# A fused decoder layer with expert retrieval: the first head searched as soon as it is scored, and a quarter of the rows scaled by ScalarE and added up by GpSimd

## What is computed

```python
def hybrid_mixer(x, ...):
    h = x @ w_in                                   # q, k, v, pooling input, gates
    o = diff_attention(q[0], q[1], k[0], k[1], v, lam, slopes)   # 8 heads, causal, ALiBi
    attn_branch = (rms_norm(o) * (1 - lam_init)) @ w_attn_proj
    pool_branch = (pooled @ pool_w * pool_scale) @ w_pool_proj
    return (g_attn * attn_branch + g_pool * pool_branch) @ w_out

def peer_ffn(y, w_q, sub_keys, u, v):              # per chunk of 128 tokens
    s = einsum(y @ w_q, sub_keys)                  # 8 retrieval heads, 2 x 128 keys
    s1, i1 = top_k(s[:, :, 0], 16); s2, i2 = top_k(s[:, :, 1], 16)
    sc, ci = top_k(s1[..., :, None] + s2[..., None, :], 16)
    idx = row * 128 + col; gate = softmax(sc)      # 128 experts per token
    act = gelu(einsum('ched,cd->che', u[idx], y))
    return einsum('che,ched->cd', gate * act, v[idx])

h = layer_norm(ALPHA * h + hybrid_mixer(h)); h = layer_norm(ALPHA * h + peer_ffn(h))
```

## Time and profile before

| | |
|---|---|
| median of 3 runs | 3364.09 us (3360.29 to 3366.54) |
| profiled execution | 3356.24 us, span 3354.3 us |
| granted clock of PE, mean | 0.957 |
| PE busy | 2827.1 us, 84% of the span |
| DVE busy | 2472.8 us, 74% |
| ACT busy | 1159.0 us, 35% |
| POOL busy | 1349.3 us, 40% |
| gathers' queue | 1073.81 MB, 79.1% of the time of 16 engines |
| other loads and stores | 169.11 MB, 13.5% |
| HBM read and written | 371 GB/s over the span |

### The profile page before, as it was taken

One profiled execution on the slowest core, in us unless ns is written; L12 is line 12 of the kernel. 1 busy time (PEld: TensorE's weight loads), 2 busy tenths in 40 slices (PEclk: granted clock), 3 DMA queues, 4 the chain that ended last, 5 costly groups with the idle time before them and its releaser, 6 DMA issues.

```text
span 3354.3 us, 30283 instructions
## 1 busy us (share of the span) xinstructions
PE 2827.1 (84%) x8384; PEld 1455.2 (43%) x8384; DVE 2472.8 (74%) x5985; ACT 1159.0 (35%) x3421; POOL 1349.3 (40%) x1248
## 2 busy tenths in 40 slices
PE   9998899899987799888988989867977777777776
PEld 7775465454533345444544534323433222222222
DVE  2312788997788868998799977798787676667664
ACT  2201355453222233445454522232323333333332
POOL 1100344465344433444454544344354444444442
PEclk9999899999998899999999989889989999999999
DMA  5631899999999999999999999999999999999997
GB/s 195 243 141 64 304 376 373 378 368 410 401 404 418 421 420 401 400 362 367 346 363 370 368 420 419 383 400 421 421 421 418 422 420 414 416 417 420 416 417 310
DMA packets 205223, 1244.97 MB, mean 371 GB/s; under 512 B 23680, under 2 KB 36992, under 8 KB 73600
## 3 DMA queue, kind: packets, MB, share of 16 engines
q0 software_dynamic: 147456, 1073.81, 79.1%
q1 hardware_dynamic: 56592, 169.11, 13.5%
q10 hardware_dynamic: 1008, 0.14, 0.0%
HBM read 1228.81 MB, written 14.16 MB: 371 GB/s over the span
## 4 chain that ended last, share of the span: by engine, by line
PE 41%; DMA 30%; DVE 18%; issue 6%; ACT 4%; POOL 1%; SPq 0%; DVEq 0%; POOLq 0%; ACTq 0%
DMA ring<-uv,idx 29%; PE r_o L1569 15%; PE w_ps L1361 14%; DVE ring L1293 7%; DVE z_e L1245 4%; PE w_ps L1481 2%; PE r_o L1539 1%; PE w_ps L1409 1%; PE w_ps L1504 1%; DVE e L1009 1%; PE w_ps L1539 1%; PE w_ps L1446 1%; PE w_ps L1486 1%; POOL ring L690 1%; PE r_o L1481 1%
## 5 line engine op out<-in xcount | busy, mean ns | idle before, releaser
L690 POOL DMA_INDIRECT ring<-uv,idx x1024 | 1191.3, 1163 | 1708.9 <-PE r_o L1569 1240.9
L1569 PE MATMUL r_o<-ring,diag 128*128 128x512 f32 x2952 | 1468.9, 631 | 407.2 <-ACT diag L879 393.7
L1293 DVE CUSTOM_DVE_ANT_0 ring<-ring,ytok 128x1024 f32<-128x1024 f32 x768 | 937.4, 1221 | 217.1 <-DMA ring<-uv,idx 216.0
L1569 PEld LDWEIGHTS r_o<-ring,diag 128*128 128x128 f32 x2952 | 548.2, 197 | 1141.7 <-ACT diag L879 595.6
L866 ACT ACTIVATE gel<-dot 128x2 f32<-128x2 f32 x512 | 104.1, 203 | 1620.6 <-DVE dot L1293 1615.7
L1361 PE MATMUL w_ps<-x,w 128*128 128x384 f32 (+1 forms) x2112 | 654.8, 456 | 7.0 <-DMA x<-xT 5.5
L1361 PEld LDWEIGHTS w_ps<-x,w 128*128 128x128 f32 x2112 | 396.3, 192 | 228.3 <-issue 57.6
L1293 DVE CUSTOM_DVE_ANT_0 ring<-ring,zn 128x1024 f32<-128x1024 f32 x256 | 313.5, 1225 | 212.2 <-DMA ring<-uv,idx 212.1
L1245 DVE SCALAR_TENSOR_TENSOR z_e<-ring,coef,z_e 128x1024 f32<-128x1024 f32 x286 | 367.4, 1285 | 7.7 <-ACT coef L870 7.7
L879 ACT ACTIVATE diag<-ident,coef 128x128 f32<-128x128 f32 x738 | 264.0, 387 | 0.0
L870 ACT ACTIVATE coef<-gel,gate 128x1 f32<-128x1 f32 x1024 | 246.0, 287 | 16.8
(11 more groups left out here) (199 smaller groups left out, 2337.3 us busy)
## 6 DMA issues: line engine op xcount, KB each, us to landing
w<-w_in SPq DMA_DIRECT2D x132, 512.0 KB, 3.7
wq<-wq SPq DMA_DIRECT2D x46, 512.0 KB, 7.8
wc<-w_branch SPq DMA_DIRECT2D x24, 768.0 KB, 5.2
ring<-uv,idx POOLq DMA_INDIRECT x1024
wo<-w_out SPq DMA_DIRECT2D x24, 512.0 KB, 12.1
xs<-x SPq DMA_DIRECT2D x8, 512.0 KB
out<-yn_e SPq DMA_DIRECT2D x8, 512.0 KB
x<-xT SPq DMA_DIRECT2D x16, 192.0 KB, 5.5
```

The lines of the kernel that those rows point to most:

```text
L690: nc.gpsimd.indirect_dma_start(out=ring[t % RING][:], out_offset=None, in_=a["uv"], in_offset=bass.IndirectOffsetOnAxis(ap=idx[:, slot:slo ...
L1293: nc.vector.tensor_tensor_reduce(ring[r][:, 0:D], ring[r][:, 0:D], y_of(n)[:], 1.0, 0.0, ALU.mult, ALU.add, dot[:, slot:slot + 1]).then_in ...
L1569: ins = nc.tensor.matmul(o_ps[n % 2][half][:], diag[(u - 1) % DIAGS][:], ring[t % RING][:, D + half * HALF:D + (half + 1) * HALF], start=s ...
```

## The change

The schedule: `SCORES_AT` and `HEAD_LEN` are replaced by a list of times for each head, `SCORE_TIMES`. Group 0's first heads are scored at -16, -9 and -2, close together, and the others more spread out, up to 72. Group 1's scoring begins at 216 instead of 203 and group 2's at 595 instead of 587, and with them their attention, branches and norms (group 1's attention at slot 7 instead of -6). Of group 1's first units two are due at -23 and -21, before the first query, and the other five between -8 and 3. Two helpers, `evacuated_at` and `pooled_at`, move ACT's and PE's pieces for group 1's second unit back by some slots.

The search: DVE carries out what is due up to the third query (-9), searches head 0, and only then does the rest up to -1. ACT takes head 0's exponent after what is due up to -4. Each later head is searched 24 slots ahead instead of 32; head 1 in slots 0 to 5 of tile 0, three steps in each.

The rows: `by_pool(t)` takes slots with t % 4 == 2, in tile 0 from slot 3 on and in later tiles from slot 72 on, up to slot 123 of the tile, before slot 723. For such a row ACT multiplies the `v` half in the ring buffer with the coefficient, in place, in place of making `diag`; POOL adds it to a new SBUF tile `zp` (`sum_row`; the first of a tile is a copy), right after the gather of slot t + 7; DVE adds `zp` to `z` once for each tile (`add_pooled`, slot 5 of the next tile). The next gather into that buffer waits for `psummed`. `by_vector` now reaches slot 723 as well. In numbers: 85 rows for POOL (30, 13, 13, 13, 13, 3 in tiles 0 to 5), 290 for DVE, 649 for PE.

The diff, without the semaphores' names and the places in SP's, ACT's and PE's parts where only the new time functions are called:

```diff
@@ -41,10 +41,10 @@
 GROUP = 2
 DIAGS = 4
 NEG = -3.0e38
-LEAD = 2
 PE_AHEAD = 2
+SEARCH_AHEAD = 24
 STEPS_AT = [2 if j < 5 else 1 if j < 13 else 0 for j in range(TOPK)]
-LATE_STEPS = [2 if 6 <= j < 15 else 0 for j in range(TOPK)]
+LATE_STEPS = [3 if 8 <= j < 14 else 0 for j in range(TOPK)]
 PAD = 16
 CA, CP = H, PG
 NP, NGATE = PG, 2 * DC
...
@@ -76,19 +76,18 @@
 STEP = (6, 5, 7)
 BRANCH_LEN = (9, 4, 6)
 NORM_LEN = (12, 7, 9)
-HEAD_LEN = (10, 12, 16)
-SCORES_AT = (-28, 203, 587)
+SCORE_TIMES = ((-16, -9, -2, 7, 20, 33, 46, 59, 72), tuple(range(216, 216 + 12 * RH + 1, 12)),
+               tuple(range(595, 595 + 16 * RH + 1, 16)))
 DRAIN = (19, 23, 23)
-T_N = tuple(SCORES_AT[g] - 15 - NORM_LEN[g] * GTS[g] for g in range(NG))
+T_N = tuple(SCORE_TIMES[g][0] - 15 - NORM_LEN[g] * GTS[g] for g in range(NG))
 T_B = tuple(T_N[g] - 3 - BRANCH_LEN[g] * DC for g in range(NG))
 T_A = tuple(T_B[g] - DRAIN[g] - STEP[g] * (NSTEPS[g] - 1) for g in range(NG))
 FIRST_UNITS = (tuple(T_A[0] - 30 + 4 * i for i in range(7)),
-               (-64, -55, -46, -37, -28, -20, -12),
+               (-23, -21, -8, -3, -1, 1, 3),
                tuple(T_A[2] - 30 + 4 * i for i in range(7)))
 LAST_UNITS = ((0, 2, 5, 7, 10, 12, 15, 17, 20),) + (tuple(range(0, 27, 3)),) * 2
 HEAD_UNITS = ((0, 3, 6, 9), (0, 3, 6, 11), (0, 5, 10, 16))
 EARLY = T_A[0] + 30
-PARKED = (T0S[1] + 1, T0S[1] + 2)
 PARKED = (T0S[1] + 1, T0S[1] + 2)
 
 DO_LOGIT = (1, 1, 1)
...
@@ -122,6 +121,14 @@
     return UNIT_T[g][i]
 
 
+def evacuated_at(g, i):
+    return unit_at(g, i) + (2 if g else 3) + (4 if (g, i) == (1, 1) else 0)
+
+
+def pooled_at(g, i):
+    return unit_at(g, i) + (13 if (g, i) == (1, 1) else 7)
+
+
 def step_at(g, k):
     return T_A[g] + STEP[g] * k
 
...
@@ -135,7 +142,18 @@
 
 
 def score_at(g, h):
-    return SCORES_AT[g] + HEAD_LEN[g] * h
+    return SCORE_TIMES[g][h]
+
+
+def query_at(g, i):
+
+    begin, end = SCORE_TIMES[g][i // 2:i // 2 + 2]
+    return begin + (end - begin) // 2 * (i % 2)
+
+
+def query_len(g, i):
+    begin, end = SCORE_TIMES[g][i // 2:i // 2 + 2]
+    return (end - begin) // 2
 
 
 def tile_of(g, k):
...
@@ -204,11 +222,29 @@
     return t % 2 == 1 and t < score_at(NG - 1, RH)
 
 
-PE_SUMS = list(itertools.accumulate(0 if by_vector(t) else 1 for t in range(LAST_SLOT)))
-DVE_SUMS = list(itertools.accumulate(1 if by_vector(t) else 0 for t in range(LAST_SLOT)))
+def by_pool(t):
+    if not (72 if t >= SLOTS else 3) <= t % SLOTS < SLOTS - 4:
+        return False
+    return t % 4 == 2 and t < score_at(NG - 1, RH)
+
+
+def by_tensor(t):
+    return not by_vector(t) and not by_pool(t)
+
+
+PE_SUMS = list(itertools.accumulate(by_tensor(t) for t in range(LAST_SLOT)))
+DVE_SUMS = list(itertools.accumulate(by_vector(t) for t in range(LAST_SLOT)))
+POOL_SUMS = list(itertools.accumulate(by_pool(t) for t in range(LAST_SLOT)))
 
 
 BASED = [n for n in range(TT) if any(by_vector(t) for t in range(SLOTS * n, SLOTS * (n + 1)))]
+POOLED = [n for n in BASED if any(by_pool(t) for t in range(SLOTS * n, SLOTS * (n + 1)))]
+
+
+def bases(n):
+
+    return sum(1 + (m in POOLED) for m in BASED if m < n)
+
 
 
 class Place:
...
@@ -670,6 +706,20 @@
         def stage(g):
             return merged(roots(g), first_norms(g))
 
+        def first_of_tile(t):
+            return not any(by_pool(j) for j in range(t // SLOTS * SLOTS, t))
+
+        def sum_row(t):
+            pool.wait_ge(row_scaled, POOL_SUMS[t])
+            row = ring[t % RING][:, D:]
+            if first_of_tile(t):
+                if t >= SLOTS:
+                    pool.wait_ge(stored, 16 * (t // SLOTS))
+                nc.gpsimd.tensor_copy(zp[:], row).then_inc(psummed, 1)
+            else:
+                pool.wait_ge(psummed, POOL_SUMS[t] - 1)
+                nc.gpsimd.tensor_tensor(zp[:], zp[:], row, ALU.add).then_inc(psummed, 1)
+
         def root(n):
             pool.wait_ge(stat_step, 4 * n + 4)
             nc.gpsimd.tensor_tensor(rstd, var, mhalf, ALU.pow).then_inc(rstd_ready, 1)
...
@@ -685,11 +735,15 @@
                 if t >= RING:
                     if by_vector(t - RING):
                         pool.wait_ge(vsummed, DVE_SUMS[t - RING])
+                    elif by_pool(t - RING):
+                        pool.wait_ge(psummed, POOL_SUMS[t - RING])
                     else:
                         pool.wait_ge(summed, PE_SUMS[t - RING])
                 nc.gpsimd.indirect_dma_start(
                     out=ring[t % RING][:], out_offset=None, in_=a["uv"],
                     in_offset=bass.IndirectOffsetOnAxis(ap=idx[:, slot:slot + 1], axis=0)).then_inc(row_in[t % RING], 16)
+                if t >= RING and by_pool(t - RING + 1):
+                    sum_row(t - RING + 1)
                 advance(t - RING)
                 if n and slot == 20:
                     root(n - 1)
...
@@ -870,7 +921,7 @@
                 nc.scalar.activation(coef[:, slot + j:slot + j + 1], gel[:, slot + j:slot + j + 1], ACT.Copy,
                                      scale=gate[:, h, e_:e_ + 1]).then_inc(coef_ready, 1)
             for j in range(GROUP):
-                if by_vector(t + j):
+                if not by_tensor(t + j):
                     continue
                 u = PE_SUMS[t + j] - 1
                 act.wait_ge(coef_ready, t + j + 1)
@@ -878,6 +929,11 @@
                     act.wait_ge(summed, u - DIAGS + 1)
                 nc.scalar.activation(diag[u % DIAGS][:], ident[:], ACT.Copy,
                                      scale=coef[:, slot + j:slot + j + 1]).then_inc(diag_ready, 1)
+            for j in range(GROUP):
+                if by_pool(t + j):
+                    act.wait_ge(coef_ready, t + j + 1)
+                    row = ring[(t + j) % RING][:, D:]
+                    nc.scalar.activation(row, row, ACT.Copy, scale=coef[:, slot + j:slot + j + 1]).then_inc(row_scaled, 1)
 
         act.dma_start(bg[:], a["b_gate"]).then_inc(small_in, 16)
         act.dma_start(psc[:], a["pool_scale"]).then_inc(small_in, 16)
...
@@ -890,17 +946,17 @@
         act.wait_ge(small_in, 32)
         act.sem_inc(yn_ready, 1)
         advance = woven(all_stages(stage))
+        advance(-4)
+        exponent(0)
         advance(-1)
-        for g in range(LEAD):
-            exponent(g)
         for n in range(TT):
             for slot in range(0, SLOTS, GROUP):
                 coefficients(n, slot)
                 if n and slot == 20:
                     normalize(n - 1)
-                g = RH * n + slot // TOPK + LEAD
-                if slot % TOPK == 14 and g < RH * TT:
-                    exponent(g)
+                ahead = SLOTS * n + slot + SEARCH_AHEAD
+                if ahead % TOPK == 14 and ahead // TOPK < RH * TT:
+                    exponent(ahead // TOPK)
                 advance(SLOTS * n + slot + GROUP)
         normalize(TT - 1)
 
...
@@ -1227,6 +1283,7 @@
             cols = slice(half * HALF, (half + 1) * HALF)
             if n in BASED:
                 dve.wait_ge(vsummed, DVE_SUMS[SLOTS * (n + 1) - 1])
+                dve.wait_ge(z_based, bases(n + 1))
                 nc.vector.tensor_tensor(z[:, cols], z[:, cols], o_ps[n % 2][half][:], ALU.add).then_inc(joined, 1)
                 return
             nc.vector.scalar_tensor_tensor(z[:, cols], y_of(n)[:, cols], ALPHA, o_ps[n % 2][half][:], ALU.mult,
@@ -1236,10 +1293,15 @@
             dve.wait_ge(yn_ready, n + 1)
             nc.vector.tensor_scalar(z[:], y_of(n)[:], ALPHA, None, ALU.mult).then_inc(z_based, 1)
 
+        def add_pooled(n):
+            dve.wait_ge(vsummed, DVE_SUMS[SLOTS * (n + 1) - 1])
+            dve.wait_ge(psummed, POOL_SUMS[SLOTS * (n + 1) - 1])
+            nc.vector.tensor_tensor(z[:], z[:], zp[:], ALU.add).then_inc(z_based, 1)
+
         def add_row(t):
             n, slot = t // SLOTS, t % SLOTS
             dve.wait_ge(coef_ready, t + 1)
-            dve.wait_ge(z_based, BASED.index(n) + 1)
+            dve.wait_ge(z_based, bases(n) + 1)
             if DVE_SUMS[t] > 1:
                 dve.wait_ge(vsummed, DVE_SUMS[t] - 1)
             nc.vector.scalar_tensor_tensor(z[:], ring[t % RING][:, D:], coef[:, slot:slot + 1], z[:], ALU.mult,
...
@@ -1271,6 +1333,8 @@
             nc.vector.tensor_tensor(yn[:], yn[:], gb[:, 1], ALU.add).then_inc(ready, 1)
 
         def norm_step(n, slot):
+            if slot == 5 and n in POOLED:
+                add_pooled(n)
             if slot in (8, 9):
                 join(n, slot - 8)
             if slot in (10, 11):
...
@@ -1295,16 +1359,15 @@
 
         setup()
         advance = woven(all_stages(stage))
+        advance(query_at(0, 2))
+        dve.wait_ge(table, 3)
+        for _ in retrieve(0):
+            pass
         advance(-1)
-        dve.wait_ge(table, 3)
         dve.wait_ge(gb_in, 32)
-        for g in range(LEAD):
-            for _ in retrieve(g):
-                pass
-        for g in range(LEAD):
-            invert(g)
-        for g in range(LEAD):
-            share(g)
+        invert(0)
+        share(0)
```

(31 more changed lines are left out.)

18 lines of the change are left out of this document (9 added, 9 removed).

## The result

The changed kernel takes 3399.63 us (median of 4 executions, 3395.79 to 3401.37), the kernel before 3363.36 beside it: a ratio of 1.0106, 95% interval 1.0089 to 1.0124. It is slower by 36 us where the forecast was faster by 35, and the time lies above the range of 3276 to 3366. The profiled execution has a span of 3396.5 us at a granted clock of 0.929, against 3354.3 us at 0.957.

What follows compares the result with a forecast made beforehand. DMA was taken to bound 800 to 1300 us and 2250 us on, PE and DVE to be nearly full in 350 to 800 and 1300 to 1900. Gains 37 + 5 - 2 - 5 = 35 us gave 3329 us, range 3276 to 3366.

Steps and rivals of the forecast that it cites:

- Part 1: Start of the kernel: first gather at about 295 us, 53 earlier; PE's first row sum at 320 us.
- Rival D: Start: a misplaced unit or norm step delays the search, first gather only 10 us early; 3372 us, chance 0.05.
- The schedule shifts "nothing": Scoring moves of 13 and 8 slots only shift work inside their stages, costing nothing.
- DVE's in tiles 0, 2 and 3: Tile 0: 48 us more DVE work, stage ends 37 us earlier; tiles 2 and 3: gain 5 us.
- the price: DVE time taken by each POOL add: 1.4 us, ends 0 and 5.0.
- rival B: An add keeps DVE's two-input work out for its whole 2.1 us; 3364 us, chance 0.12.
- the forecast's own rule: 338 to 800 us: a third of DVE's added 48 us is given back, 16 us off the 53 us lead.
- PE's relief: Four passes saved, 1.72 us per pooled row: 52 us in tile 0, 45 for tiles 2 and 3.
- Covered: Tile 1, between 800 and 1300 us: DMA is full, so DVE's 18 added us cost only 0 to 3.
- Tile 4: Slots 586 to 634, 2160 to 2305 us: DVE's 129 of 145 us plus 18 is too much; 3 to 8 lost.
- rival A: PE was the one bound and POOL takes only gaps, DVE price 0: 90 us gained, 3274 us, chance 0.16.
- Rival C: POOL's queue: adds stand ahead of gathers, so refills come 2.3 us or more late; 3404 us, chance 0.09.

Runs made afterwards that it cites:

- The schedule alone: Changed kernel with no row given to POOL (PE 734 rows, DVE 290): 3327.6 us, ratio 0.9883; run again, 3322.6 us, ratio 0.9877.
- the adds on one column: Changed kernel with POOL's 79 adds cut to one column of 1024, scaling and waits kept: 3317.8 us, ratio 0.9860.
- the tail: New schedule with 25 pooled rows only in tiles 6 and 7, where DMA is full: 3329.9 us, ratio 0.9902; run again, 3327.1 us, ratio 0.9888.
- the kernel with writes: Changed kernel with each POOL add replaced by three memsets of the same length together, reading nothing from SBUF: 3319.4 us, ratio 0.9865.

## Why the prediction was wrong

**Part 1 was right.** Search at 287.52 us (forecast 285), first gather at 297.15 (295), first row sum of PE at 310.76 with 0.37 us idle before it (320, with little idle). Rival D falls.

**The schedule shifts "nothing" was wrong by some 20 us.** The schedule alone keeps 28 of its 53 us of lead in the profile, 36 by the medians. It loses 14 between slots 192 and 256, and 10 from 384 to 512 (14 and 11 in its second profile), around the places where the scoring of a group moved by 13 and 8 slots. That these moves cause it was not tried.

**The step that failed is DVE's in tiles 0, 2 and 3, twice over.** In the profiles the forecast's lead of 35 us at the end became a lag of 42. Of these 77 us 25 belong to the schedule, 19 to tile 0 (16 us given back, 35 measured), 33 to tiles 2 and 3 (5 gained, 28 lost), and 2 to the first gather; tiles 1 and 4 came out as forecast, and 2 us came back after them.

First the price: I took 1.4 us per add from a hold of 0.1 us in a row of a 128-element scaling. The runs show 1.87 per add, for an add of 2.43 us where I had 2.1. The hold was no accident: before has eleven such meetings, each with a row sum of 1.38 us. But that scaling is recorded as running for 0.54 us inside the row sum and took 0.1 us from it, while an add holds for all of its recorded length: the short row was no scale for the long one. In after, first a meeting with a product, then one in which the product was far enough ahead, in the timeline:

```profile
1066.10 4.03 DVE L1357 CUSTOM_DVE_ANT_0 ring<-ring,ytok 128x1024 f32<-128x1024 f32 x1
...
1066.68 2.35 POOL L721 TENSOR_TENSOR zp_e<-zp_e,ring 128x1024 f32<-128x1024 f32 x1
```

```profile
737.59 1.22 DVE L1357 CUSTOM_DVE_ANT_0 ring<-ring,ytok 128x1024 f32<-128x1024 f32 x1
738.39 2.62 POOL L721 TENSOR_TENSOR zp_e<-zp_e,ring 128x1024 f32<-128x1024 f32 x1
...
738.73 3.36 DVE L1307 SCALAR_TENSOR_TENSOR z_e<-ring,coef,z_e 128x1024 f32<-128x1024 f32 x1
```

Every product and row sum that met an add follows one pattern. The 34 that began during an add ended 1.08 to 1.11 us after its end. The 27 products that were under way for 0.05 to 0.58 us when an add began ended 1.09 us after its end, as if most of their 1.22 us were still to come; the 24 products and row sums that had begun 0.63 us or more ahead took their usual time, and there the add took longer (up to 2.79 us instead of 2.35) and held what came next. So a product can be held by an add that starts after it, and 0.58 + 2.36 + 1.09 = 4.03 us is the longest. A short instruction, in the first stage:

```profile
648.90 2.78 DVE L1239 TENSOR_SCALAR ab<-besti 128x16 uint32<-128x16 uint32 x1
...
649.27 2.36 POOL L721 TENSOR_TENSOR zp_e<-zp_e,ring 128x1024 f32<-128x1024 f32 x1
...
652.14 1.22 PE L1472 MATMUL w_ps<-k,q 64*128 64x512 f32 x2 [6.13 <-DVE o L1108]
```

The first line is 16 elements long, has one SBUF input, and takes 0.18 us elsewhere (293.34, in head 0's search). Here it ends with POOL's add, 2.6 us later than it would. The attention step behind it on DVE (L1108) is late by that, and PE, which waits for it, stands idle for 6.13 us, of which the hold accounts for at most 2.6. Held products, 112 of the 157 us that DVE's busy time grows by over before, are rival B's mechanism, "an add keeps DVE's two-input work out for its whole time". I gave it 0.12 and put its time at 3364, 36 us too fast. Its rule was the one of the Trainium skill, "SBUF — State Buffer", section "Who interferes with whom": a DVE instruction with two SBUF inputs contends with a GpSimd instruction that reads SBUF, not with one that only writes it, and whichever issues second is fully blocked. The runs agree with what it says of reads and of writes: products up to 4.03 us beside adds, and 1219 ns beside writes. With "second" they agree only if an add counts from some 0.6 us ahead of its recorded start; why it should was not tried. I weighed one short row against a rule that named this very case.

Second, what a DVE us is worth. This is the larger miss: by the forecast's own rule the dearer price alone would have cost another 5 us in the first stage (a third of 30 x 1.87 + 6 = 62 instead of 48). I gave back a third of DVE's added time there, 16 of 48 us. The 30 rows took 35 us of lead, PE's relief included, and the lead at slot 192 was 18.8 us, not 37. Against the adds on one column, DVE is busy for 57 us more up to slot 192 in after, and these slots take 48 us longer: five sixths, not a third. For tiles 2 and 3 I said +5, setting DVE's 36 us against 45 from PE, as if the one could pay for the other. From slot 256 to 512 after's lead fell by 38 us, the schedule's by 9: 28 us for 26 rows. Tile 2's pooled slots, 330 to 378, in the schedule alone and in after:

```profile
1343.00:1504.00 161.00, 135.42 (x447) 71.74 (x446) 144.56 (x346) 74.29 (x185) 66.89 (x63) 0.93 0.95 373
```

```profile
1380.00:1556.00 176.00, 123.41 (x403) 65.46 (x401) 160.22 (x343) 80.80 (x183) 95.04 (x74) 0.85 0.90 338
```

DVE is busy for 90% of the one and 91% of the other. Its 16 added us went straight into the length, 15 us, and the 12 us that PE was spared went into PE's idle time. An idle tenth of DVE was not to be had: of 16 us idle in the first of these stretches, DVE waited 7.3 for ACT's exponents, 6.8 for PE's attention products and 1.4 for gathered rows.

**"Covered" was right.** For tile 1 I forecast 0 to 3 us lost; against the schedule alone it is 2. From the gather of slot 202 to that of slot 250, in the schedule alone and in after:

```profile
969.00:1109.00 140.00, 95.56 (x242) 43.99 (x241) 120.02 (x254) 40.47 (x128) 55.74 (x51) 0.93 1.01 411
```

```profile
1005.00:1148.00 143.00, 83.58 (x202) 40.73 (x200) 138.78 (x256) 49.15 (x128) 94.24 (x62) 0.80 1.01 409
```

DVE has 19 us more, up to 97% busy, and the stretch is 3 us longer: the DMA engines are full (1.01), and DVE's idle time could shrink. These 13 rows cost 0.2 us each, near the 0.3 of the tail. Tile 4 (3 to 8 lost) was right too: 5.5, 0.4 per row.

**PE's relief was worth little.** With one column the kernel gains 10 us over the schedule alone, for relief and scaling together; rival A had counted on 52 in tile 0 alone. Once DVE is late, POOL waits for DVE's row sums as long as for PE's: from 350 to 800 us (total, times, longest) its waits for PE fall from the 153.8 us of the earlier trace rows, and those for DVE grow from 44.8.

```profile
POOL ring L742 <- DVE z_e L1307: 69.2, 33, 5.5
POOL ring L742 <- PE r_o L1630: 68.9, 25, 6.8
```

Where PE idles more, its granted clock is lower too: 0.92 in this stage (PE busy 374 of 450 us) against 0.97 in before (416) and 0.99 in the schedule alone (431), and 0.73 in the pooled slots of tile 4 (80 of 139 us) against 0.84 (89 of 129). So part of what PE saved in matmuls it paid back in longer ones: the row-sum matmul takes 643 ns on average, 629 in the schedule alone. How much of the 82 us goes by this way was not separated.

**Rival C named nearly the right time, 3404 us, for a wrong reason.** A number alone would have seemed to bear it out; the kernel with writes refutes it, at 3319.

The sum, by medians: schedule -36, PE's relief and the scaling -10, the adds' length, that is their reading, +82, together +36.

## What to carry to other kernels

Before work goes to GpSimd because it is idle, ask what it reads: each us of an SBUF read there took 0.6 to 0.8 us from a VectorE that works on two SBUF inputs, and about half of that reached the end. Test it with two stand-ins, one column in place of the whole, and writes of the same length in place of the read: together they tell the queue, the hold and the relief apart in two runs. Count an engine's idle time as nearly free only where the transfers are the bound (share 1.01 here): a row cost 0.2 to 0.3 us there, and 1.1 to 1.2 in the two stages where engines set the pace. Time an overlap by an operation of the length that you mean to add.

The best kernel of this study is the new schedule without pooled rows, 3327.6 and 3322.6 us in two sets of runs, 1.2% faster than before.
